# Block-diagonal gate products of a recurrence, cut into heads on four quarters of TensorE's array

## The reference

```python
def rg_lru(x, w_a, b_a, w_i, b_i, lam):
    bsz, seq, _ = x.shape
    xf = x.astype(jnp.float32)
    xh = xf.reshape(bsz, seq, LRU_HEADS, LRU_HEAD_DIM)
    r = jax.nn.sigmoid(jnp.einsum("bshi,hij->bshj", xh, w_a.astype(jnp.float32)).reshape(bsz, seq, D_LRU)
                       + b_a.astype(jnp.float32))
    i = jax.nn.sigmoid(jnp.einsum("bshi,hij->bshj", xh, w_i.astype(jnp.float32)).reshape(bsz, seq, D_LRU)
                       + b_i.astype(jnp.float32))
    log_a = LRU_C * r * jax.nn.log_sigmoid(lam.astype(jnp.float32))
    a = jnp.exp(log_a)
    mult = jnp.sqrt(-jnp.expm1(2.0 * log_a))
    u = mult * (i * xf)
    ...
    _, h = lax.associative_scan(combine, (a, u), axis=1)
    return h
```

## Time and profile before

| | us |
|---|---|
| median of 3 runs | 2539.28 |
| lowest, highest of the 3 | 2539.18, 2540.31 |
| the profiled execution: its time | 2540.26 |
| the profiled execution: its span | 2538.1 |
| TensorE busy / VectorE busy / ScalarE busy in the span | 2496.4 / 1832.2 / 1181.7 |
| mean granted TensorE clock in the span | 0.996 |

### The profile page before, as it was taken

How to read it: one execution, slowest core, us unless ns; L and a number is a source line. 1 busy time by engine, 2 the same in 40 slices (tenths; PEclk the granted TensorE clock), 3 DMA queues, 4 the chain that set the end, 5 groups by cost and what they waited for, 6 DMA issues and landing times.

```text
span 2538.1 us, 42090 instructions
## 1 busy us (share of the span) xinstructions
PE 2496.4 (98%) x15684; PEld 2174.2 (86%) x15684; DVE 1832.2 (72%) x2368; ACT 1181.7 (47%) x1442; POOL 17.5 (1%) x52
## 2 busy tenths in 40 slices
PE   7999999999999999999999999999999999999998
PEld 6888888888888888888888888888888888888887
DVE  4668989996556655787685665676788668865886
ACT  3346445544444444654444554455544444444444
POOL 0000000000000000000000000000000000000000
PEclk9999999999999999999999999999999999999999
DMA  9999977797666665566555556556555655566554
GB/s 386 404 387 354 398 255 285 242 331 242 189 187 186 190 207 171 179 208 192 180 166 174 159 187 187 183 196 190 175 196 184 191 187 178 189 199 184 184 169 126
DMA packets 167239, 556.78 MB, mean 219 GB/s; under 512 B 16577, under 2 KB 22721, under 8 KB 167121
## 3 DMA queue, kind: packets, MB, share of 16 engines
q1 hardware_dynamic: 165792, 551.94, 65.0%
q0 software_dynamic: 1328, 3.21, 0.4%
HBM read 552.47 MB, written 2.10 MB: 219 GB/s over the span
## 4 chain that ended last, share of the span: by engine, by line
PE 85%; DVE 8%; DMA 3%; issue 2%; ACT 2%; SPq 0%; DVEq 0%; ACTq 0%
PE ps L637 50%; PE ps L644 25%; DMA ride<-in_w_ada 2%; PE ps L634 2%; DVE split L1347 2%; DVE acc_ada L1413 2%; PE pm L662 1%; PE ps L641 1%; PE ps L619 1%; PE ps L621 1%; PE ps L620 1%; ACT split L994 1%; DMA x_t<-in_w_ada 1%; DVE x_t L1513 0%; DVE val L1367 0%
## 5 line engine op out<-in xcount | busy, mean ns | idle before, releaser
L1347 DVE TENSOR_TENSOR split<-raw,split 128x1024 fp32r<-128x1024 f32 (+1 forms) x864 | 1030.8, 1203 | 601.1 <-ACT split L994 596.6
L994 ACT ACTIVATE split<-raw 128x1024 fp32r<-128x1024 f32 (+1 forms) x864 | 896.4, 1043 | 1079.6 <-PE ps L644 948.2
L637 PE MATMUL ps<-h_s,split 128*128 128x512 f32 x3592 | 1134.7, 397 | 6.2 <-DVE h_s L1491 2.5
L644 PEld LDWEIGHTS ps<-h_s,split 128*128 128x128 f32 x3592 | 676.0, 188 | 159.9
L637 PE MATMUL ps<-mid_s,split 128*128 128x512 f32 x2336 | 734.8, 396 | 0.8 <-DVE split L1347 0.4
L644 PE MATMUL ps<-h_s,split 128*128 128x256 f32 x3592 | 706.7, 278 | 0.0
L637 PEld LDWEIGHTS ps<-h_s,split 128*128 128x128 f32 x3592 | 548.8, 189 | 11.1 <-issue 5.4
L644 PEld LDWEIGHTS ps<-mid_s,split 128*128 128x128 f32 x2336 | 438.8, 188 | 103.7
L644 PE MATMUL ps<-mid_s,split 128*128 128x256 f32 x2336 | 458.9, 278 | 0.0
L637 PEld LDWEIGHTS ps<-mid_s,split 128*128 128x128 f32 x2336 | 355.6, 189 | 4.3 <-issue 2.7
L1001 ACT ACTIVATE low<-ps 128x512 f32<-128x512 f32 x238 | 138.1, 580 | 18.6 <-PE ps L644 18.6
(11 more groups left out here) (281 smaller groups left out, 1483.3 us busy)
## 6 DMA issues: line engine op xcount, KB each, us to landing
raw<-in_w_in SPq DMA_DIRECT2D x224, 512.0 KB, 3.7
raw<-in_w_ffn_down SPq DMA_DIRECT2D x128, 512.0 KB, 4.3
ride<-in_w_ada SPq DMA_DIRECT2D x44, 1024.0 KB, 11.7
raw<-in_w_ffn_gate SPq DMA_DIRECT2D x88, 512.0 KB, 4.1
raw<-in_w_ffn_up SPq DMA_DIRECT2D x88, 512.0 KB, 4.3
raw<-in_w_ffn_a SPq DMA_DIRECT2D x88, 512.0 KB, 3.8
raw<-in_w_ffn_b SPq DMA_DIRECT2D x88, 512.0 KB, 4.4
raw<-in_w_out SPq DMA_DIRECT2D x64, 512.0 KB, 4.6
```

Source lines behind the costliest of these rows:

```text
L637: pe.matmul(ps[:, s, b, :], split[:, slot, k, 0, b * P:(b + 1) * P], acts[:, k0 + k, :, :].rearrange("p h t -> p (h t)"), start=start, sto ...
L644: mm = pe.matmul(ps[:, s, b, 0:T], split[:, slot, k, 1, b * P:(b + 1) * P], acts[:, k0 + k, 0, :], start=False, stop=stop)
L994: act.activation(split[:, c, 0:kt, 0, :], raw[:, CHUNKS * s + c, 0:kt, :], ACT.Copy).then_inc(hi_ready, 1)
L1347: dve.tensor_tensor(split[:, c, 0:kt, 1, :], raw[:, CHUNKS * s + c, 0:kt, :], split[:, c, 0:kt, 0, :].bitcast(F32), ALU.subtract).then_inc ...
```

## The change

`gates` no longer multiplies by whole 128 x 128 blocks. Each product is cut into its two heads, 64 rows by 64 columns: the head h takes rows 64h to 64h+63 of the array. The results of `rg_a` go to the same partitions as their head, those of `rg_i` to the other half ("turned"), so that the four small products of a block fill the four quarters of the array. Results of head 0 go to bank `pm0`, those of head 1 to `pm1`; the two blocks of a call stand side by side along the free axis. `gates_mm` is raised twice a call, by the last product of each head, and `sigmoids` waits for both.

`sigmoids` has eight activations a call instead of four, each on 64 partitions; those of `gate_i` read one half of the partitions and write the other. Since the bias is read at the partitions of the input, a turned copy of `b_rg_i`, `bias_i`, is loaded by two more DMAs on GpSimd's queue behind those of `rg_a` and `rg_i`, and `gates(0)` waits for six loads instead of four. `bias_i` takes 32 bytes ahead of `inv_n`, so `inv_n`, the small sums, `ssq`, `rstd` and everything at `F` lie 32 bytes further on.

```diff
     lam_n8 = at("lam_n8", [P, LB], place(32))
+    bias_i = at("bias_i", [P, LB], place(32))
     inv_n = at("inv_n", [P, 16], place(64))
...
+    def half_rows(h):
+        return slice(LRU_HEAD * h, LRU_HEAD * (h + 1))
...
+        first = PARAMS["b_rg_i"][0]
+        for h in range(2):
+            pool.dma_start(bias_i[half_rows(1 - h), :], dram["params"][half_rows(h), first:first + LB]).then_inc(side_loaded, 16)
         pool.wait_ge(chunk_used, HALF_CHUNKS + 6)
...
             if q == 0:
-                pe.wait_ge(side_loaded, 16 * 4)
+                pe.wait_ge(side_loaded, 16 * 6)
             if q >= 1:
                 pe.wait_ge(gates_read, q)
             for b in range(2):
                 blk = 2 * q + b
-                pe.matmul(pm[b][:, 0:T], rg_a[:, blk, :], xc[:, blk, :], start=True, stop=True)
-                mm = pe.matmul(pm[b][:, T:2 * T], rg_i[:, blk, :], xc[:, blk, :], start=True, stop=True)
-            mm.then_inc(gates_mm, 1)
+                for w, turned in ((rg_a, False), (rg_i, True)):
+                    for h in range(2):
+                        rows, cols = half_rows(h), half_rows(1 - h if turned else h)
+                        mm = pe.matmul(pm[h][cols, b * T:(b + 1) * T], w[rows, blk, rows], xc[rows, blk, :], start=True, stop=True)
+                        if b == 1 and turned:
+                            mm.then_inc(gates_mm, 1)
...
         def sigmoids(q):
-            act.wait_ge(gates_mm, q + 1)
+            act.wait_ge(gates_mm, 2 * q + 2)
             for b in range(2):
-                blk = 2 * q + b
-                act.activation(gate_r[:, blk, :], pm[b][:, 0:T], ACT.Sigmoid, bias=col("b_rg_a", blk))
-                last = act.activation(gate_i[:, blk, :], pm[b][:, T:2 * T], ACT.Sigmoid, bias=col("b_rg_i", blk))
+                blk, cols = 2 * q + b, slice(b * T, (b + 1) * T)
+                for h in range(2):
+                    rows, turned = half_rows(h), half_rows(1 - h)
+                    act.activation(gate_r[rows, blk, :], pm[h][rows, cols], ACT.Sigmoid, bias=col("b_rg_a", blk)[rows])
+                    last = act.activation(gate_i[rows, blk, :], pm[h][turned, cols], ACT.Sigmoid,
+                                          bias=bias_i[turned, blk:blk + 1])
             last.then_inc(gates_read, 1)
```

## The result

| | before | after |
|---|---|---|
| median of the runs, us | 2540.47 (2539.11 to 2541.11) | 2545.67 (2544.16 to 2546.91) |
| profiled execution, us | 2540.26 | 2544.16 |
| its span, us | 2538.1 | 2542.3 |
| chain of waits, share of TensorE and of DMA | 85%, 3% | 86%, 3% |

The ratio of the times is 1.0022 [1.0015, 1.0029], thirteen runs of each on one chip. The kernel became 5.2 us slower, where 1.2 us faster was forecast, and the time lies above the range.

The account below looks back on a forecast made before the run. TensorE's own work was taken as the bound (85% of the span), with a DMA wait between the pairs of gate calls. Calls one and two 0, three and four -1.17: 2539.28 - 1.17 = 2538.1 us, range 2536.8 to 2541.0.

Parts of the forecast that it names:

- the term for the shifted addresses: Buffers at F moving by 32 bytes: the sum counts "nothing else" beside the gate calls, so no cost.
- Loads at shifted addresses get dearer: Rival, chance 0.09: loads into the two moved `ride` slots cost 0.5 to 3.2 us more; 2538.6 to 2541.3.
- Clock in the longer wait: Rival, chance 0.27: TensorE's clock falls in the longer wait before 171.9 us, losing 1.5 us; 2539.6.
- The gates: Each gate call's products take 0.86 us instead of 1.72, less shape changes; 1.17 us saved per pair of calls.
- two at a time: Rival, chance 0.09: only two array quarters run together, calls stay at 1.72 us plus shape changes; +0.55, 2539.8.
- one after another: Rival, chance 0.06: the small gate products do not overlap, a call takes 3.44 us; +6.5, 2545.8.
- Calls one and two worth nothing: Time saved ahead of the ride's fourth piece, landing at 171.85, only lengthens TensorE's wait from 1.45 to 2.62 us.
- All four calls pay: Rival, chance 0.05: the fourth ride piece comes earlier along with TensorE, so the first pair's gain counts too; 2536.9.
- The cover of 0.15: ScalarE's idle time left per call after eight sigmoids take 3.0 us instead of 1.57; cost taken as zero.
- The small loads: Two added loads on GpSimd's queue land by 139.3, needed at 152.5 us; cost zero.
- the third rival: The rival "one after another", chance 0.06, 2545.8, left outside the range.
- the unnamed cases: Outcomes no rival names, chance 0.04, half of it slower by over 0.2%.

Follow-up runs that it names:

- the idle products: Changed kernel plus three and four TensorE products nobody reads, in the waits before the ride's third and fourth piece: 2543.52 against 2544.84 us without them.
- the first experiment: The whole change, but `bias_i` behind the last buffer so that no other tile moves, against the kernel before: 2539.88 against 2540.33 us, ratio 1.0001.

## Why the prediction was wrong

**The step that failed** is the term for the shifted addresses. The sum has "nothing else" behind the gates, so it puts this term at 0; the shift alone measured +4.66. As a rival, "Loads at shifted addresses get dearer", the prediction had named the right mechanism and the right buffer, and then went wrong three times.
- It was given 0.09 with the reason "Nothing in the trace speaks for it; all loads there have round addresses". The trace of before couldn't speak for it or against it, since it holds one layout only; and the second half was false. `raw`, `x_t` and `ride_2` lie 128 bytes off a multiple of 256. The 0.09 was worked out from no row, and one look at the addresses in the code would have taken the reason away.
- It priced only the bytes that go to the two moved slots, 51 us of full DMA, at up to one part in sixteen, 3.2 us. The sixteen came from rows of 4 KB, but 16 of the 20 loads go out in rows of 2 KB. What happened is 3% of all bytes: 405 to 393 GB/s, with the unmoved `raw` slower as well (161.6 to 164.3 ns a packet). From 36 us to the wait near 172 the DMA engines are full nearly all the time, and 136 x 0.03 = 4.1 us, an estimate, beside the 4.08 measured. (That it meets it so closely owes something to where the stretch is taken to begin.)
- So the range ended at 2541.0, below this rival's own upper figure of 2541.3.

The Trainium skill, in "DMA: Bandwidth & Descriptors", section "How a descriptor splits into AXI transactions", has transactions start on a grid of 256 bytes, so that a descriptor that starts off it takes one more. In kind this agrees with the runs: the layout with all on 256 is the fastest. In size it doesn't: 17 for 16 would make a packet of 4 KB 6% longer and 9 for 8 one of 2 KB 12%, estimates from that page, and from all on 256 to the layout after they went up by 3% and 4% (159.2 to 164.3 and 84.4 to 88.1 ns). The section also counts beats of 32 bytes; by these a start 128 off would cost a 2 KB packet four beats and one 32 off only one, of 64, estimates again, while both gave 393 GB/s. And the rule says nothing of packets to another buffer, which slowed too.

**Clock in the longer wait** was given 0.27 and a price of 1.5 us. Without the shift the waits were forecast at 1.1 and 1.5 and came at 1.18 and 1.51; the fall came at 171.7; its price is 1.1 to 1.4. What the prediction missed is that this rival and the shift don't exclude each other. The shift is shown to cost 4.7 us, more than the gates give back; that the clock costs the slower executions of the changed kernel the 1.3 us that the idle products took away is the likeliest reading, not one that a profile shows.

**The gates** came out nearly as worked out. The second call after the change, TensorE's timeline:

```profile
162.85 0.28 PE L628 MATMUL ps<-h_s,split 128*128 128x256 f32 x1
163.06 0.43 PE L787 MATMUL pm<-xc,rg_a 64*64 64x256 f32 x2
163.08 0.43 PE L787 MATMUL pm<-xc,rg_i 64*64 64x256 f32 x2
163.33 0.38 PE L787 MATMUL pm<-xc,rg_a 64*64 64x256 f32 x2
...
164.09 0.39 PE L626 MATMUL ps<-h_s,split 128*128 128x256 f32 x1
164.31 0.28 PE L627 MATMUL ps<-h_s,split 128*128 128x256 f32 x1
```

From 162.85 to 163.06 stands 0.21 us, of it 0.09 for the change of shape. Four products start together, those of `rg_i` 0.02 behind those of `rg_a`, and the next four 0.27 later (163.06 to 163.33), or 0.21 to 0.22 thereafter. So all four quarters do run beside each other, and "two at a time" and "one after another" fall. The measured 2545.67 lies beside the 2545.8 of "one after another"; that is chance, for the calls became shorter and not longer. The Trainium skill's rule that row and column groups compose ("TensorE: Matmul & The Clock Gate", "Part 3: Packing small matmuls — row/col tiling") holds in these rows. The call takes 164.31 - 163.06 - 0.12 = 1.13 us, where 0.86 + 0.23 = 1.09 was forecast. By the offsets the third call saved 4.08 - 3.38 = 0.70 (forecast 0.63) and the fourth, with the 0.09 on its way in, 3.38 - 2.88 = 0.50 (0.54).

**Calls one and two worth nothing** held, with all landings 4 us later. The timeline after, the third and fourth piece:

```profile
173.43 1.04 PE L669 MATMUL pm<-x_t,c_act 128*1 128x256 f32 x16 [1.49 <-DMA x_t<-in_w_ada]
175.99 1.04 PE L669 MATMUL pm<-x_t,c_act 128*1 128x256 f32 x16 [1.51 <-DMA x_t<-in_w_ada]
```

The fourth started at 171.90 before and starts at 175.99 now. "All four calls pay" falls.

**ScalarE** was right in its effect and wrong in its number. The timeline of ScalarE at the first call, the first and the last sigmoids:

```profile
157.28 0.47 ACT L1104 ACTIVATE gate_r<-pm,par 64x256 f32<-64x256 f32 x1 [1.11 <-PE pm L787]
157.76 0.47 ACT L1105 ACTIVATE gate_i<-pm,bias_i 64x256 f32<-64x256 f32 x1
...
160.66 0.47 ACT L1105 ACTIVATE gate_i<-pm,bias_i 64x256 f32<-64x256 f32 x1
161.16 1.06 ACT L1004 ACTIVATE split<-raw 128x1024 fp32r<-128x1024 f32 x1
```

The sigmoids start 0.48 apart, not 0.36: here the next one doesn't start before the one ahead has ended. Eight take 3.9 us instead of 3.0. The cover of 0.15 is exceeded by some 0.7 a call, and the conversion follows without idle time. The ring of converted chunks took this up: of TensorE's waits from 173 to 335 us only the two for VectorE are left beside those for the two pieces, as before, and none for a conversion.

```profile
PE pm L669 <- DMA x_t<-in_w_ada: 3.0, 2, 1.5
...
PE pm L800 <- DVE mid_s L1690: 0.6, 1, 0.6
...
PE ps L644 <- DVE mid_s L1663: 0.3, 1, 0.3
```

"PSUM Bottleneck" in the Trainium skill's "TensorEngine Tiling (Array Packing)" warns that packing doesn't speed up the readers of PSUM. Their time grew more than worked out, from 1.57 to 3.9 us a call, and still did not reach TensorE.

**The small loads** cost nothing, as forecast. GpSimd's issue of `bias_i`, and the landing times of its two loads:

```profile
133.76 1.06 POOL L583 DMA_DIRECT2D bias_i<-in_params  x2
```

```profile
DMA to landing us min/median/max: 7.5/7.8/8.2
```

They land by some 142 us, and the first sigmoid starts at 157.28.

**The chance of "slower" by over 0.2%** was 0.08, and the ratio of 1.0022 is on that side, if barely. Only the third rival and the unnamed cases had been put there; the shift alone reaches 1.0020.

**What stays open.** Why unmoved loads become slower with `ride` isn't settled: the runs show that it is so, not by which part of the chip; nor is which packets of before took longer, with most of them at the shortest time. The fall of the clock near 172 us was seen in one profile only, that of the first experiment. A part of the difference comes late: between 1000 us and the end the offset grows from 2.9 to 3.9 us without a stretch to which it could be put. The offset of the shift without `ride` grows by 0.8 there as well, so that it need not belong to the change. Whether the sigmoids are 0.48 apart for their 64 partitions, or because the second gate reads one half of the partitions and writes the other, wasn't separated.

## What to carry to other kernels

When a change takes a buffer, however small, work out the new address of every buffer behind it, and look at which of them are targets of loads in a stretch that the DMA limits; an unknown that the trace can't show is worth one run before it gets a low chance. In a stretch bound by DMA, try the targets of large loads on multiples of 256 bytes, all of them: here that was worth 4.3 us, more than the four calls could give on the path together. And time taken from an engine ahead of a transfer's landing is a longer wait, in which the clock may fall: add that price, don't set it against the others.

## What the runs showed of the hardware

- The start of a load's target, 32, 64 or 128 bytes off a multiple of 256, costs pace: 393 GB/s with `ride` off as well, 405 with the tiles from `raw` on (`raw` and `ride_2` among them) off by 128 and `ride` on it, 410 with all on it. The loads whose targets had not moved slowed too; with all on it, 99.7% of the packets of 2 KB took 84 ns, with all off 26%.
- Four products of 64 rows and 64 columns in float32 run on the four quarters at once: the 16 matmul instructions of a call (two to a product) take 0.86 us, and 0.27 more go by around them. Changing the shape of the array costs 0.09 on the way in and 0.2 to 0.3 on the way out.
- Sigmoids of 64 x 256, by turns from the same partitions and from the other half, start 0.48 us apart where those of 128 x 256 start 0.36 apart.
- With TensorE busy 1.48 of 3.6 us the clock fell to 1.2 GHz for 3.4 us in one profiled execution; in that of the changed kernel, with TensorE busy 1.19 of 3.2 us, it stayed at 2.4. Idle products in the two waits kept it at 2.4 GHz, worth 1.1 to 1.4 us where it had fallen, and cost 0.8 us in a kernel whose profile shows no fall there.
